# A two-block transformer kernel: the attention layers' stages put in another order

## The chip, the core and the metric

The kernel runs on one core of a Trainium2 chip. The time is the device time of the whole program in microseconds (us). The core has a matrix engine, TensorE (PE in the profile, its weight loads PEld), VectorE (DVE), ScalarE (ACT), GpSimd (POOL) and SyncE (SP), which here only issues DMAs. Each engine takes its own instructions strictly in the order in which they were written, and they meet through semaphores. TensorE writes to eight PSUM banks of 128 x 512 f32.

## What is computed

A sequence of 256 tokens of width 1024 goes through two layers of a first block (`_layer`, twice) and through a second block (retention, a SwiGLU, a short convolution, eight experts). Everything is f32. The change is inside `_layer`, ahead of its feed-forward part:

```python
xn = _rms(x, norm_mix_g)
z = xn @ w_in                       # 1024 x 7756 weights
(m_qk, m_v, m_o, m_if, s_q, s_ckv, i_q, i_k, i_w, d_q, d_k, d_v, g_pre) = _split_cols(z)
# branch a: mLSTM. Causal convolution and silu on m_qk, chunked decays from m_if,
y_a = sigmoid(m_o) * _rms(_mlstm(mq, mk, m_v, m_if + gate_b))
# branch b: sparse attention. 64 keys a query, chosen by an index score
kv = _rms(s_ckv) @ w_kv_up
y_b = _dsa(rope(_rms(s_q)), rope(_rms(kv_k)), kv_v, rope(i_q), rope(i_k), i_w)
# branch c: difference of two softmaxes
y_c = _rms(_diff_attn(rope(_rms(d_q)), rope(_rms(d_k)), d_v, lam)) * (1 - lam_init)
gates = sigmoid(g_pre + b_gate)     # three of 1024 columns
merged = sum(gates[i] * (y[i] @ w_branch[i]) for i in range(3))
x = x + merged @ w_out
```

## The kernel before

The program is one function, `build`, with a block of instructions for each engine. The order of each engine is written out by hand; nothing plans it. Tokens are tiled in two (`tt`) of 128. Weights come through a ring of six units of 1 MB that SP loads in the order of use and that waits for the unit six earlier to be read (`stream`, `unit_read`). `chunk` (L564) is the usual projection: two units, for each `tt` one bank and eight matmuls, then ScalarE copies the bank to `z` (`z_evac`). A gate chunk has one more matmul for its bias.

Banks go round: `fill(ALL)` takes the next of the eight and first waits until whoever was handed that bank eight fills ago has emptied it. `hand(ins, bank, who)` gives a filled bank to ScalarE or VectorE, which take theirs in that order. `point(name)` marks how many banks had been handed over, and others wait until all up to there are emptied. `transposes` (L448) turns four 128 x 128 tiles into one bank.

TensorE's order in a layer (`layer`, L706) before: `norm_transposes`; the eight columns of `m_if` from a small resident weight `w_if` (two groups of eight matmuls, 4 rows out); `m_qk` feature-major (two chunks); eight `z_chunks` (v, o, and six of 438 columns from s_q to d_v); two gate chunks; transposes of the normed `s_ckv`; the kv up-projection; two gate chunks; all of the mLSTM (`mlstm`, L852, ending with transposes of its output); transposes of the heads of s_q, k, d_q, d_k, i_q and i_k; the index scores; six banks of sparse scores; one gate chunk; transposes of the probabilities and products with the values; transposes of y_b; six banks of the differential scores; the last gate chunk; the differential weights' transposes and products; transposes of y_c; the three branch projections (L835 on); `w_out`; the feed-forward part.

VectorE's (`layer`, L1733): `mlstm_rows` and `convolve`; then, once ScalarE has emptied all z chunks (`point("z")`), the squares of s_q, d_q, d_k and s_ckv, one root for all, `rope` of s_q; `ckvT`; `rope` of d_q, d_k, i_q, i_k and of the keys; `mlstm`, which ends with `out_norm` and the product with the sigmoid; `top_keys` (L1686 on: sums the index scores, then eight rounds of MAX8 and MATCH_REPLACE8 for each `tt`); `scores` (mask, maximum, for each of six banks); the output of the sparse branch; `scores` again, the difference of the two softmaxes, `out_norm`; the merging of the branches. ScalarE evacuates banks, and takes the exponentials (`exps`), roots and, in one go at the end, the sigmoid of all 3072 gate columns. On ScalarE a change between functions such as Exp, Ln, Sqrt, Silu and Sigmoid shows as an ACT_TABLE_LOAD.

Of the kernel before, what the change touches and what calls it, by code (L numbers as in the profile page):

```python
# [10 lines left out]
ALU = mybir.AluOpType  # L11
ACT = mybir.ActivationFunctionType
AX = mybir.AxisListType

P = 128
# [30 lines left out]
PARAMS = 24  # L46
# [59 lines left out]
def build(nc, a, out):  # L106

    ctx = ExitStack()
    with ctx:
# [11 lines left out]
        w_if = sb("w_if", [P, DEPTH, KT, 8])  # L121
# [16 lines left out]
        rowf = ybuf[0:M_HEADS, 4 * SEQ:12 * SEQ].rearrange("p (r t) -> p r t", t=SEQ)  # L138
# [132 lines left out]
        sig_act = signal("sigmoids")  # L271
# [35 lines left out]
        gates_after = dict(z=2, kv=2, mlstm=0, dsa=1, diff=1)  # L307
# [22 lines left out]
        z_chunks = [(C_V, 512), (C_O, 512)] + [(C_SQ + 438 * i, 438) for i in range(6)]  # L330
        g_chunks = [(C_G + 512 * i, 512) for i in range(6)]
# [10 lines left out]
        def _(eng):  # L342
# [363 lines left out]
            def layer(li):  # L706
# [12 lines left out]
                for _, n in z_chunks:  # L719
                    chunk(n, "act")  # L720
                point("z")
                g_left = [list(range(6))]

                def gates(m):

                    for c in range(m):
                        i = g_left[0].pop(0)
                        pe_bias = li * 6 + i
                        chunk(512, "act", bias=pe_bias)

                gates(gates_after["z"])
# [15 lines left out]
                gates(gates_after["kv"])  # L747
                mlstm()
                gates(gates_after["mlstm"])

                eng.wait_ge(rope_dve.sem, pe.next(rope_dve))
                for col in (C_SQ, None, C_DQ, C_DK):
                    for half in range(2):
                        def src(i):
                            c = (2 * half + i // 2) * P
                            return kv[:, i % 2, c:c + P] if col is None else zc(i % 2, col + c, P)
                        transposes(src, 4, "act")
                transposes(lambda i: zc(i % 2, C_IQ + (i // 2) * P, P), 4, "act")
                transposes(lambda i: tmp[:, 3, i * P:(i + 1) * P], 2, "act")
                point("heads")  # L760
                eng.wait_ge(act_freed.sem, pe.point("heads", act_freed))

# [9 lines left out]
                for which in (0, 2):  # L772


                    for j in range(6):
# [7 lines left out]
                    if which == 0:  # L783
                        gates(gates_after["dsa"])

                        def turn_probs(j):
                            eng.wait_ge(prob_act.sem, 12 * li + j + 1)
                            transposes(lambda i: pbuf[:, j, i * P:(i + 1) * P], 4, "act")
                            point("pT")


                        turn_probs(0)
                        for j in range(6):
                            tt, _, hs = score_bank(j)
                            if j < 5:
                                turn_probs(j + 1)
                            if j in (0, 2):
                                bo = fill(ALL)
                            eng.wait_ge(act_freed.sem, pe.point("pT", act_freed))
                            for i, h in enumerate(hs):  # L800
                                for s in range(tt + 1):
                                    c = (i * (tt + 1) + s) * P
# [1401 lines left out]
```

## Time and profile before

| | |
|---|---|
| median of three runs | 2911.97 us (2903.65 to 2913.78) |
| the profiled execution | 2908.88 us |
| its span, first to last instruction | 2907.1 us |
| mean granted TensorE clock | 0.962 |
| PE busy | 2704.9 us (93%) |
| DVE, ACT, POOL busy | 1802.8, 1177.7, 231.9 us |
| DMA | 610 MB, 210 GB/s on average |
| first layer, from the first projection to the merged branches | 34 to 411 us |
| the same of the second layer | 655 to 1035 us |

The span is cut into stretches by time from its start. "Busy" of an engine is the time in which it had an instruction; the granted clock (PEclk) is the share of TensorE's full clock that it was given, 1.00 for 2.4 GHz and 0.50 for 1.2 GHz.

### The profile page before, as it was taken

What the parts mean: (1) busy time and instruction counts of PE and PEld (TensorE: products, weight loads), DVE (VectorE), ACT (ScalarE), POOL (GpSimd) and SP (SyncE); (2) the same over time, 40 slices, a digit from 0 to 9 for tenths busy, and PEclk for the clock granted to TensorE, in tenths of its full rate; (3) what the DMA queues carried; (4) which work ended last, traced back from release to release, by engine and by line L of the source; (5) the groups of instructions that cost most, each with busy time, mean ns of one, the idle gap of its engine ahead of it and who ended that gap; (6) DMA issues with size and microseconds to landing.
All of it is one profiled execution on the core that took longest, in us unless ns stands there. A gap on an engine that the chain in (4) does not pass through costs nothing.

```text
span 2907.1 us, 29086 instructions
## 1 busy us (share of the span) xinstructions
PE 2704.9 (93%) x11636; PEld 2037.4 (70%) x11636; DVE 1802.8 (62%) x1938; ACT 1177.7 (41%) x1325; POOL 231.9 (8%) x112
## 2 busy tenths in 40 slices
PE   5997898989997889989989989799999999999997
PEld 4445546876445448888768879687878778787876
DVE  2045525442065345555555447699999989999997
ACT  1112311011113310034620014577777777777775
POOL 0000003320000013300024320000000000000000
PEclk9998899999997899999999999899999999999999
DMA  5441135532430145545445535498989989898985
GB/s 161 139 158 58 58 116 174 201 132 101 164 130 30 58 161 186 201 140 177 157 148 207 193 120 186 146 381 311 381 318 361 338 323 372 313 382 315 376 328 195
DMA packets 276201, 610.10 MB, mean 210 GB/s; under 512 B 12670, under 2 KB 50228, under 8 KB 275904
## 3 DMA queue, kind: packets, MB, share of 16 engines
q1 hardware_dynamic: 276032, 607.64, 59.0%
q8 instruction: 131, 2.15, 0.3%
q14 instruction: 38, 0.31, 0.0%
HBM read 606.56 MB, written 1.05 MB: 209 GB/s over the span
## 4 chain that ended last, share of the span: by engine, by line
PE 83%; DVE 12%; ACT 3%; issue 1%; SPq 0%; DMA 0%; DVEq 0%; ACTq 0%
PE bank L418 81%; DVE split L1455 5%; PE bank L448 2%; PE bank L637 1%; DVE parts L1501 1%; ACT xs L1077 1%; DVE x_resid L1483 1%; DVE work L1712 0%; ACT split L1077 0%; DVE parts L1441 0%; DVE top L1711 0%; DVE tmp L1491 0%; ACT parts L1077 0%; SPq L2044 0%; ACT L1077 0%
## 5 line engine op out<-in xcount | busy, mean ns | idle before, releaser
L418 PE MATMUL bank<-split,parts 128*128 128x512 f32 (+1 forms) x6720 | 1539.7, 389 | 29.3 <-DVE parts L1441 13.1
L418 PEld LDWEIGHTS bank<-split,parts 128*128 128x128 f32 x6720 | 1247.7, 189 | 291.5 <-issue 19.8
L1455 DVE TENSOR_TENSOR split<-ring,split 128x2048 fp32r<-128x2048 f32 x444 | 1024.5, 2353 | 95.2 <-POOL split L2025 67.7
L1077 ACT ACTIVATE split<-ring 128x2048 fp32r<-128x2048 f32 x336 | 641.8, 1918 | 194.9 <-PE bank L418 194.9
L418 PE MATMUL bank<-ring,xnT 128*128 128x512 f32 (+1 forms) x1024 | 428.9, 578 | 1.8 <-ACT xnT L1077 1.8
L418 PEld LDWEIGHTS bank<-ring,xnT 128*128 128x128 f32 x1024 | 194.3, 192 | 234.2 <-issue 231.9
L2025 POOL TENSOR_SCALAR split<-ring 128x2048 fp32r<-128x2048 f32 x108 | 231.7, 2148 | 1477.6 <-DVE x_resid L1483 1114.3
L1077 ACT ACTIVATE parts<-bank 128x512 fp32r<-128x512 f32 x150 | 79.7, 583 | 390.5 <-PE bank L637 390.5
L1501 DVE TENSOR_TENSOR parts<-bank,parts 128x512 fp32r<-128x512 f32 x150 | 95.4, 678 | 144.3 <-ACT parts L1077 144.3
L1077 ACT ACTIVATE tmp<-bank 128x512 f32<-128x512 f32 x158 | 87.6, 586 | 203.6 <-PE bank L418 203.6
L1491 DVE TENSOR_TENSOR tmp<-bank,tmp 128x512 f32<-128x512 f32 x150 | 97.8, 679 | 115.7 <-PE bank L418 114.8
L1469 DVE TENSOR_TENSOR halves<-ring,halves 128x1024 fp32r<-128x1024 f32 x96 | 116.4, 1224 | 79.3 <-ACT halves L1077 78.8
L1077 ACT ACTIVATE halves<-ring 128x1024 fp32r<-128x1024 f32 x96 | 101.3, 1060 | 144.0 <-PE bank L418 144.0
L1077 ACT ACTIVATE z<-bank 128x512 f32<-128x512 f32 (+1 forms) x52 | 29.0, 566 | 223.6 <-PE bank L418 223.6
L418 PE MATMUL bank<-xparts,halves 128*128 128x256 f32 x960 | 116.8, 285 | 0.3 <-DVE xparts L1441 0.3
L418 PEld LDWEIGHTS bank<-xparts,halves 128*128 128x128 f32 x960 | 116.4, 193 | 0.9 <-issue 0.9
L1555 DVE TENSOR_TENSOR tmp<-z 128x512 f32<-128x512 f32 (+1 forms) x16 | 10.0, 626 | 156.2 <-ACT z L1077 155.8
L1483 DVE TENSOR_TENSOR x_resid<-bank,x_resid 128x512 f32<-128x512 f32 x60 | 41.3, 692 | 91.1 <-PE bank L418 91.1
L418 PE MATMUL bank<-ring,ybuf 128*128 128x512 f32 x192 | 88.4, 624 | 1.6 <-ACT ybuf L1077 1.6
L418 PE MATMUL bank<-halves,xparts 128*128 128x512 f32 x384 | 88.6, 391 | 0.0
L448 PE MATMUL bank<-const,xs 128*128 128x128 f32 x176 | 34.7, 378 | 55.1 <-ACT xs L1077 52.1
L418 PEld LDWEIGHTS bank<-halves,xparts 128*128 128x128 f32 x384 | 71.8, 188 | 15.1 <-issue 0.5
(233 smaller groups left out, 1619.9 us busy)
## 6 DMA issues: line engine op xcount, KB each, us to landing
ring<-in_moe_w_gate SPq DMA_DIRECT2D x112, 1024.0 KB, 7.9
ring<-in_moe_w_up SPq DMA_DIRECT2D x112, 1024.0 KB, 7.5
ring<-in_moe_w_down SPq DMA_DIRECT2D x112, 1024.0 KB, 7.5
ring<-in_w_gate_up SPq DMA_DIRECT2D x44, 1024.0 KB, 5.2
ring<-in_w_in SPq DMA_DIRECT2D x40, 1024.0 KB, 6.3
ring<-in_ret_w_in SPq DMA_DIRECT2D x24, 1024.0 KB, 5.1
ring<-in_w_down SPq DMA_DIRECT2D x22, 1024.0 KB, 5.0
ring<-in_w_in SPq DMA_DIRECT2D x24, 876.0 KB, 5.8
```

Source lines behind the costliest of these rows:

```text
L418: return nc.tensor.matmul(o, l, r, start=first, stop=final, **kw)
L448: ins = nc.tensor.transpose(bank[b][:, i * P:i * P + rows], src_of(i), ident[0:rows, 0:rows])
L637: return [nc.tensor.transpose(bank[b[tt]][:, f * P:(f + 1) * P], hb[:, tt, f * P:(f + 1) * P], ident) for f in range(n // P)]
L1077: return nc.scalar.activation(out, in_, func, **kw)
L1455: V.tensor_tensor(split[:, m % SPLITS, 1, :], ring[:, n % RING, :], split[:, m % SPLITS, 0, :].bitcast(F32), ALU.subtract).then_inc(low_ma ...
L1469: V.tensor_tensor(low, half_of(n, j, by_column), high.bitcast(F32), ALU.subtract).then_inc(half_low.sem, half_low.tick())
L1483: ins = V.tensor_tensor(o, b[:, :], o, ALU.add)
L1491: ins = V.tensor_tensor(hb[:, tt, 0:n], b[:, 0:n], sg[:, tt, 0:n], ALU.mult)
L1501: V.tensor_tensor(parts[:, 1, f, c], b[:, 0:n].rearrange("p (f t) -> p f t", t=P), parts[:, 0, f, c].bitcast(F32), ALU.subtract).then_inc( ...
L1555: then(V.tensor_tensor(sq, src, src, ALU.mult))
L2025: nc.gpsimd.tensor_scalar(split[:, m % SPLITS, 0, :], ring[:, n % RING, :], 1.0, 0.0, ALU.mult, ALU.add).then_inc(high_made.sem, high_made ...
```

## The change

Nothing is computed otherwise; the stages stand in another order on each engine, and some are cut finer.

The small weight `w_if` and its two loads go. The columns from `m_if` to `d_v` are now six chunks of 440 (436 the last), so that `m_if` comes out token-major with s_q, and four small matmuls against the identity turn it. The new order of TensorE in a layer is: m_qk; the chunk with s_ckv; the index chunk; transposes of normed s_ckv; the chunk with m_if and s_q; kv up-projection; `m_if` turned; index heads turned; v; index scores; o; sparse heads turned; chunk dq; sparse scores; chunks dk and dv; gates 1; probabilities and values of the sparse branch; the mLSTM's exponents and weights; y_b turned; differential heads turned; branch 1; the mLSTM's values; gates 0; y_a turned; differential scores; gates 2; differential products; branch 0; y_c turned; branch 2. VectorE norms and turns heads as each chunk comes, sums the index scores and chooses keys before it scans the mLSTM's rows, and merges a branch as it comes (`merge`). ScalarE takes the sigmoids straight from the banks (`z_evac` with a function). SP loads the weights in the new order.

```diff
-        w_if = sb("w_if", [P, DEPTH, KT, 8])
-        z_chunks = [(C_V, 512), (C_O, 512)] + [(C_SQ + 438 * i, 438) for i in range(6)]
-        g_chunks = [(C_G + 512 * i, 512) for i in range(6)]
+        z_v, z_o = (C_V, 512), (C_O, 512)
+        z_if_sq, z_ckv, z_index, z_dq, z_dk, z_dv = [(C_IF + 440 * i, min(440, C_G - C_IF - 440 * i)) for i in range(6)]
...
@@ tensor, layer @@
-                b = fill(ALL)
-                for g in range(2):
-                    for k in range(KT):
-                        ins = mm(bank[b][0:4, g * SEQ:(g + 1) * SEQ], w_if[:, li, k, 4 * g:4 * g + 4], xnT[:, k, :],
-                                 k == 0, k == KT - 1)
-                hand(ins, b, "dve")
...
+                columns(z_ckv, "ckv")
+                columns(z_index, "index")
                 eng.wait_ge(kvn_dve.sem, pe.next(kvn_dve))
                 transposes(lambda i: yb[:, i % 2, (i // 2) * P:(i // 2 + 1) * P], 4, "dve")
                 point("ckvT")
+                columns(z_if_sq, "sq")
...
+                eng.wait_ge(act_freed.sem, pe.point("sq", act_freed))
+                b = fill(ALL)
+                for g in range(2):
+                    for tt in range(TT):
+                        c = g * SEQ + tt * P
+                        ins = mm(bank[b][0:4, c:c + P], zc(tt, C_IF + 4 * g, 4), ident, True, True)
+                hand(ins, b, "dve")
...
+                columns(z_v, "v")
+                eng.wait_ge(act_freed.sem, pe.point("index heads", act_freed))
                 for tt in range(TT):
                     for odd in range(2):
                         b = fill(ALL)
...
+                columns(z_o, "o")
+                turn_heads(lambda tt, c: zc(tt, C_SQ + c, P), lambda tt, c: kv[:, tt, c:c + P])
+                columns(z_dq, "dq")
+                head_scores(0)
+                columns(z_dk, "dk")
+                columns(z_dv, "dv")
+                gates(1)
...
+                mlstm_weights()
+                eng.wait_ge(dve_freed.sem, pe.point("dsa", dve_freed))
+                turn_branch()
+                turn_heads(lambda tt, c: zc(tt, C_DQ + c, P), lambda tt, c: zc(tt, C_DK + c, P))
+                branch(1)
+                mlstm_values()
+                gates(0)
+                eng.wait_ge(yb_dve.sem, pe.next(yb_dve))
+                turn_branch()
+                head_scores(2)
+                gates(2)
+                eng.wait_ge(act_freed.sem, pe.point("dv", act_freed))
...
+                branch(0)
+                eng.wait_ge(yb_dve.sem, pe.next(yb_dve))
+                turn_branch()
+                branch(2)
@@ scalar, layer @@
+                z_evac(*z_ckv)
+                for f in range(KT):
+                    eng.wait_ge(conv_dve.sem, act.next(conv_dve))
+                    A(mqkT[:, f, :], mqkT[:, f, :], ACT.Silu).then_inc(silu_act.sem, silu_act.tick())
+                head_roots(24, 25)
+                z_evac(*z_index)
+                z_evac(*z_if_sq)
+                head_roots(0, 8)
...
+                z_evac(*z_o, ACT.Sigmoid)
+                turned_heads(0)
+                z_evac(*z_dq)
                 exps()
-                gates(gates_after["dsa"])
+                z_evac(*z_dk)
+                z_evac(*z_dv)
+                head_roots(8, 24)
+                gates(1)
...
-                for tt in range(TT):
-                    A(zc(tt, C_G, 3 * D), zc(tt, C_G, 3 * D), ACT.Sigmoid).then_inc(sig_act.sem, sig_act.tick())
@@ vector, layer @@
-                eng.wait_ge(act_freed.sem, dve.point("z", act_freed))
+                eng.wait_ge(act_freed.sem, dve.point("ckv", act_freed))
+                z_sums(((3, (C_CKV, 1, 256)),))
...
+                eng.wait_ge(act_freed.sem, dve.point("sq", act_freed))
+                z_sums(((0, (C_SQ, 8, HD)),))
+                mean_squares(z_heads(1, 0, 8), z_heads(0, 0, 8), HD)
+                z_inverse(0, 8)
+                rope_from_z(C_SQ, 0)
+                mlstm_rows(li)
                 eng.wait_ge(act_freed.sem, dve.point("kv", act_freed))
...
-                mlstm()
                 top_keys()
                 scores(lambda tt: msel[:, 0:P] if tt == 0 else msel[:, P:384])
+                mlstm_scans()
+                eng.wait_ge(act_freed.sem, dve.point("dq", act_freed))
+                z_sums(((1, (C_DQ, 8, HD)),))
+                eng.wait_ge(act_freed.sem, dve.point("dk", act_freed))
+                z_sums(((2, (C_DK, 8, HD)),))
...
+                mlstm_weights()
+                merge(1, True)
+                mlstm_values()
                 scores(lambda tt: const[:, K_DIAG:K_DIAG + P] if tt == 0 else causal2)
...
+                merge(0, False)
+                ins = merge(2, False)
@@ sync @@
-            for li in range(DEPTH):
-                load(w_if[:, li, :, :], a["w_in"][li, :, C_IF:C_IF + 8].rearrange("(k p) c -> p k c", p=P))
             load(w_rt[:, :, :], a["moe_router_2"].rearrange("(k p) c -> p k c", p=P))
...
+                for col, width in (z_ckv, z_index, z_if_sq):
                     columns(w_in, col, width)
-                gate_columns(gates_after["z"])
                 rows_of(a["dsa_w_kv_up"][li], 1)
+                for col, width in (z_v, z_o, z_dq, z_dk, z_dv):
+                    columns(w_in, col, width)
+                gates(1)
+                branch(1)
+                gates(0)
+                gates(2)
+                branch(0)
+                branch(2)
                 rows_of(a["w_out"][li], 4)
```

## Rows read from the trace of the kernel before

**Rows 1.** The page, part 1: busy time, share and instructions of each engine.
```profile
PE 2704.9 (93%) x11636; PEld 2037.4 (70%) x11636; DVE 1802.8 (62%) x1938; ACT 1177.7 (41%) x1325; POOL 231.9 (8%) x112
```

**Rows 2.** Waits of TensorE, 34 to 1036 us, both layers: total, times, longest.
```profile
PE bank L448 <- DVE yb L1684: 18.9, 2, 9.5
PE bank L418 <- DVE tmp L1699: 13.3, 2, 6.6
...
PE bank L448 <- DVE yb L1651: 11.4, 2, 5.7
PE bank L418 <- ACT pT L1077: 10.7, 8, 3.2
...
PE bank L418 <- ACT ikT L1077: 2.2, 2, 1.1
PE bank L418 <- DVE ckvT L1763: 2.1, 2, 1.0
...
PE bank L448 <- DVE yb L1789: 1.6, 2, 0.8
```

**Rows 3.** Windows: stretch, length, busy (instructions) of engines, PEclk, DMA share, GB/s.
```profile
240.00:244.50 4.50, 4.50 (x25) 3.36 (x23) 1.28 (x3) 2.61 (x4) 0.00 (x0) 1.00 0.65 208
244.50:259.20 14.70, 14.70 (x53) 12.34 (x52) 5.93 (x19) 2.85 (x4) 0.00 (x0) 0.54 0.19 79
268.70:272.00 3.30, 3.30 (x16) 3.30 (x17) 0.00 (x0) 2.13 (x5) 0.00 (x0) 0.52 0.00 0
272.00:281.30 9.30, 8.18 (x80) 7.52 (x78) 3.59 (x13) 5.73 (x11) 0.00 (x0) 1.00 0.01 2
288.00:296.00 8.00, 8.00 (x10) 3.03 (x11) 7.41 (x23) 0.00 (x0) 0.00 (x0) 0.51 0.00 0
312.20:333.00 20.80, 20.02 (x102) 19.50 (x103) 4.38 (x8) 5.55 (x17) 0.00 (x0) 0.52 0.14 56
350.00:357.00 7.00, 4.86 (x37) 3.95 (x35) 0.69 (x1) 3.50 (x5) 0.00 (x0) 1.00 0.82 298
362.70:369.00 6.30, 5.52 (x13) 3.06 (x14) 0.00 (x0) 4.99 (x4) 0.00 (x0) 0.50 0.01 4
...
936.70:957.30 20.60, 19.75 (x101) 19.26 (x103) 4.17 (x7) 5.39 (x16) 0.00 (x0) 0.52 0.14 56
```

**Rows 4.** Timeline of TensorE, first layer: start, length, instructions.
```profile
34.02 7.07 PE L418 MATMUL bank<-xnT,w_if 128*4 128x256 f32 x32 [1.06 <-DVE xnT L1420]
...
68.75 98.27 PE L418 MATMUL bank<-ring,xnT 128*128 128x512 f32 x256
166.94 1.12 PE L418 MATMUL bank<-bgate,const 12*128 12x512 f32 x2
...
272.90 2.35 PE L448 MATMUL bank<-const,z 128*128 128x128 f32 x20
...
365.41 44.16 PE L418 MATMUL bank<-ring,ybuf 128*128 128x512 f32 x96 [0.78 <-ACT ybuf L1077]
```

**Rows 5.** Timeline of ScalarE, first layer: one load of a function table.
```profile
83.29 1.28 ACT L1077 ACT_TABLE_LOAD   x1
```

**Rows 6.** Timeline of VectorE, first layer: row sums, norm and rope of keys, key selection.
```profile
41.44 0.46 DVE L1610 TENSOR_SCALAR ybuf<-bank,gateb 4x256 f32<-4x256 f32 x1
...
221.05 0.69 DVE L1555 TENSOR_TENSOR tmp<-xs 128x512 f32<-128x512 f32 x1
...
231.36 0.69 DVE L1576 TENSOR_TENSOR xs<-tmp 128x512 f32<-128x512 f32 x1
...
277.33 0.35 DVE L1699 TENSOR_SCALAR idx<-bank,iw 128x128 f32<-128x128 f32 x1 [8.70 <-PE bank L418]
...
287.35 0.48 DVE L1699 TENSOR_SCALAR tmp<-bank,iw 128x256 f32<-128x256 f32 x1
```

**Rows 7.** Timeline of SP at the start: issues of the last parameters.
```profile
9.89 2.31 SPq L2044 DMA_DIRECT2D w_if<-in_w_in x2
12.23 6.09 SPq L2044 DMA_DIRECT2D w_rt<-in_moe_router x1
```

**Rows 8.** Chain of waits at the start, and DMA packets from 18 to 20.3 us.
```profile
12.23 8.00 DMA w_rt<-in_moe_router
...
DMA packets 2669, 0.16 MB, mean 70 GB/s; under 512 B 2631, under 2 KB 2631, under 8 KB 2669
```

More of the change, by code:

```diff
@@ L45 @@
 HALVES = 4
-PARAMS = 24
+PARAMS = 22
 GROUPS = D_FF // HALF
@@ L718, in layer, with columns, gates @@
                     point("qk")
[L719 to L731, printed above, removed]
+                def columns(z_chunk, name=None):
+                    chunk(z_chunk[1], "act")
+                    if name:
+                        point(name)
+                def gates(branch):
+                    for i in range(2):
+                        chunk(512, "act", bias=6 * li + 2 * branch + i)
+                    point("gates")
+                columns(z_ckv, "ckv")
+                columns(z_index, "index")
                 eng.wait_ge(kvn_dve.sem, pe.next(kvn_dve))
@@ L771, in layer, with turn_heads, head_scores @@
                         hand(ins, b, "dve")
-                for which in (0, 2):
+                def turn_heads(q_of, k_of):
+                    eng.wait_ge(rope_dve.sem, pe.next(rope_dve, 2))
+                    for of in (q_of, k_of):
+                        for half in range(2):
+                            transposes(lambda i: of(i % 2, (2 * half + i // 2) * P), 4, "act")
+                    point("heads")
+                def head_scores(which):
+                    eng.wait_ge(act_freed.sem, pe.point("heads", act_freed))
                     for j in range(6):
@@ L828, in layer, with branch @@
                                    "act")
[L829 to L833 removed]
+                    point("branch")
+                def branch(br):
+                    eng.wait_ge(act_freed.sem, pe.point("branch", act_freed))
                     views = [take((2, 1024)), take((2, 1024))]
@@ L884, in mlstm @@
                     hand(ins, b, "dve")
-                eng.wait_ge(yb_dve.sem, pe.next(yb_dve))
-                for half in range(2):
-                    transposes(lambda i: yb[:, i % 2, (2 * half + i // 2) * P:(2 * half + i // 2 + 1) * P], 4, "act")
             for li in range(DEPTH):
@@ L1256, in layer, with gates, head_roots @@
-                copy(iqT[:, :, :].rearrange("p f t -> p (f t)"))
-                copy(ikT[:, :], SEQ)
+                        b = take()
+                        A(zc(tt, col, n), b[:, 0:n], func).then_inc(act_freed.sem, act_freed.tick())
+                def gates(branch):
+                    for i in range(2):
+                        z_evac(C_G + (2 * branch + i) * HALF, HALF, ACT.Sigmoid)
+                def head_roots(lo, hi):
+                    o, i = (hsum[:, r, kA:kB].rearrange("p (t c) -> p t c", t=TT)[:, :, lo:hi] for r in (2, 1))
+                    roots(o, i)
@@ L1259, in exps, with turned_heads @@
+                def turned_heads(first):
+                    for w in (first, first + 1):
+                        for half in range(2):
+                            copy(hT4[:, w, 2 * half:2 * half + 2, :].rearrange("p f t -> p (f t)"))
                 def exps():
@@ new lines, in z_sums, with z_inverse, rope_from_z @@
+                def z_sums(cols):
+                    for tt in range(TT):
+                        o = kA + 25 * tt
+                        for i, (col, nh, w) in cols:
+                            heads_sum(heads(zc(tt, col, nh * w), nh), nh, w, hsum[:, 0, o + 8 * i:o + 8 * i + nh])
+                def z_inverse(lo, hi):
+                    eng.wait_ge(root.sem, dve.next(root))
+                    then(V.reciprocal(z_heads(3, lo, hi), z_heads(2, lo, hi)))
+                def rope_from_z(col, i):
+                    for tt in range(TT):
+                        c = kA + 25 * tt + 8 * i
+                        rope(zc(tt, col, 512), 8, tt, hsum[:, 3, c:c + 8], qk_gain[:, (0, 2, 3)[i], li, :],
+                             done=rope_dve if tt else None)
```

292 lines of the change are left out of this document (121 added, 171 removed).

## The prediction

> **What bounds the kernel now.** I read the page first: TensorE is busy 93% of the span and no other engine is above 62% [rows 1], so a change that leaves the arithmetic alone can only win where TensorE waits, where its clock is low, or where its work goes. The page's slices put nearly all of the low ones in the two attention stretches, 34 to 411 and 655 to 1035 us. There I read, in this order, the list of TensorE's waits, which names each and its releaser; the windows, for the granted clock; and the timelines of TensorE, VectorE and SP, to lay out the new order by the durations of the old. The rest of the program isn't touched, and I carry it over unchanged.
>
> The reader should see two losses of about the same size. The first is waiting. Per layer TensorE waits 9.5 us for the mLSTM's output norm, 6.6 us for a bank that VectorE still holds while it sums the index scores (L1699), 5.7 us for the norm of the differential output, 3.2 us for the first probabilities, and 1.1, 1.0 and 0.8 us for smaller things [rows 2]. The second is the clock. It is at 1.2 GHz (0.50 to 0.54) in five stretches of the first layer [rows 3], and the second layer has their twins, one of which stands there, at 0.52 in 936.7 to 957.3 us.
>
> **Part 1: the waits.** The sum over both layers of those that the new order covers is 18.9 + 13.3 + 11.4 + 2.2 + 2.1 + 1.6 = 49.5 us, and of the 10.7 us on `pT` the two first ones, 6.4 us, so 55.9 us or **28.0 a layer** [rows 2]. What covers each in the new order:
> - mLSTM output norm (9.5): `mlstm_values` is followed by gates 0, two chunks. A chunk of 512 costs 98.27 us / 3652 columns x 512 = 13.8 us (eight z chunks are 2 x 512 + 6 x 438 columns), and with two biases of 1.1 us a gate chunk is 16 us, so the pair covers with 32 us a VectorE chain that is under 12.
> - differential output norm (5.7): branch 0 stands there, a third of 44.16 us [rows 4], under 14 at full clock.
> - first probabilities (3.2): three stages stand between scores and probabilities (dk, dv, gates 1), some 56 us.
> - `ckvT`, `ikT`, y_b (2.9 together): a projection or the mLSTM's weights follow each.
> - the differential weights: they were hidden behind one gate chunk but for the `pT` copies; now two chunks stand there.
>
> The three later `pT` waits (0.7 each), the wait of 0.8 us for the last branch's transposes and that of 1.5 us for the merge stay.
>
> **Part 2: the bank.** The 6.6 us come from the ring of eight banks. The index scores' four banks are VectorE's, and the third is free only once it reaches L1699 of the second token tile, 287.35 + 0.48 - 277.33 = 10.5 us after it begins [rows 6]. In the new order the fill that meets this bank is the first of chunk dq. From the end of the s_q chunk TensorE needs until then: kv up-projection 7.1, m_if turned 0.9, index heads 0.7, v 13.8, index scores 1.4, o 13.8, sixteen transposes 1.9 (2.35 us for 20 [rows 4]), in all 39.6 us. VectorE needs from the same moment: evacuation 0.6, norm and rope of s_q 11.0 (the same work as 221.05 to 232.05 on the keys), three operations on four rows, 1.4, norm and rope of the keys 11.0, about 2 for three table loads that ScalarE has ahead of that root (1.28 each [rows 5], part of it under the sums), and the 10.5 [rows 6]: 36.5 us. So there are 3 us to spare, and I count no wait. It is the tightest place of the new order; each microsecond that VectorE is later than that would be one of TensorE, twice. The other chains have more: the heads of the sparse branch are ready 11 us early, the differential ones 30.
>
> **Part 3: the clock.** TensorE time lost to 1.2 GHz a layer is busy time x (1 - clock): 14.70 x 0.46 + 3.30 x 0.48 + 8.00 x 0.49 + 20.02 x 0.48 + 5.52 x 0.50 = **24.6 us** [rows 3]. Three of these stretches follow a wait that goes: those at 288 and 362.7 follow waits of 6.6 and 5.7 us and hold dense work, and 312.2 begins behind the 3.2. But the first, 244.5 to 259.2, follows none: TensorE was busy for all of 240 to 244.5, with the mLSTM's four-row matmuls, and the clock fell. So not everything comes back. In the new order the sparse probabilities and values, the mLSTM's weights, and 24 transposes follow one another: at full clock 7.3 (half of the 12.9 us of their stage inside 312.2 to 333, and one set of transposes), 9.5 (four heads of 2.3 us and the rows' transpose), 0.9 and 1.9 us. Counting from the row, the mLSTM's weights hold the full clock for about 4.5 us; the other 5 cost double, the transposes after it 1.6 more (as in 268.7 to 272), and some of branch 1 perhaps runs low, up to half of 4 us: **8 us a layer come back as a new loss**. Bounds: none, if the clock holds, and 16, if it falls already under the probabilities (3.3 + 9.5 + 3). I take 8 because that is what the only row with such matmuls behind a dense stage shows; behind the new small stages elsewhere (index scores, heads, differential products) I take none, since like ones ran at 1.00 in 272 to 281.3 and 350 to 357.
>
> The Trainium skill, "TensorE: Matmul & The Clock Gate", section "HAM oscillation — how this bites in real kernels", names gaps in which the array is idle as what gates the clock. By that the new stretch, which has no gap, would keep 2.4 GHz, and the loss of 8 would be none; the row at 240 to 244.5, busy throughout and followed by 0.54, speaks against it [rows 3].
>
> **Part 4: work removed.** The 32 instructions on `w_if` take 7.07 us [rows 4], in the second layer too, apart from the clock there, which the next stage would take over. In their place come eight instructions of a transpose's size, 0.9 us (bounds 0.5 to 1.6: 2.35 us for 20, and double), and eight more columns, 0.2 us. **6.0 us a layer.**
>
> **Part 5: ScalarE and DMA.** With sigmoids taken per stage, ScalarE changes its function table 15 times a layer where it did 10 times: 5 x 1.28 = 6.4 us more [rows 5]. I cost them at nothing: ScalarE is idle for most of a layer, and the two that lie on a chain (ahead of the keys' root) are in part 2. The Trainium skill, "ScalarE: Activation LUTs", section "Table sets: the hidden batching unit", asks for calls to be batched by set, which the change undoes; if each stood in TensorE's way it would cost 12.8 us in all, and the sum would be that much worse. The SP queue issues the same units in a new order, the ring stays six deep, and no wait of TensorE in rows 2 is for weights; nothing.
>
> **Part 6: the start.** Nothing starts until the last parameter has landed, at 20.2 us, 8.00 us after the issue of the router weights [rows 8]. The two `w_if` loads before them take 2.31 us of SP's queue [rows 7] and are, like the router's, made of 32-byte pieces, 1024 each. The router's issue moves up by 2.3 us; 2048 pieces fewer at the rate of 18 to 20.3 us (2631 in 2.3) give 1.8 more: **4.1 us**. Bounds: 0, if other parameters decide, and 7.6, if the 8.00 us shrink by two thirds.
>
> **The sum.** 4.1 + 2 x (28.0 + 24.6 + 6.0 - 8) = 4.1 + 2 x 50.6 = 105.3 us. The profiled execution took 2908.88 us, 1.8 more than its span, and gives 2803.6. It lies 3.1 us below the median of the runs, 2911.97, by which the forecast is 2806.7: I say 2806.
>
> **Rivals.**
> - *The clock holds* (the page's rule): 2 x 8 us better, about 2790. For it: dense work now stands on both sides. Against it: the row at 240 to 244.5.
> - *The clock falls early*, under the sparse probabilities: 2 x 8 worse, about 2822. For it: in 312.2 to 333 the same stage, TensorE busy, stayed at 0.52 for its whole length. Against: it entered that stage behind a wait.
> - *The bank's wait only moves* to chunk dq, or the change doesn't cover what it says elsewhere: VectorE 6 us later than in part 2 costs 3 us a layer, and 10 later 7; 2812 to 2820.
> - *Slower than before*: the clock falls in the stretch of small matmuls and stays at 1.2 GHz through the dense stages behind it. From gates 1 to the merge there are 145 us of TensorE work at full clock in a layer; all of it low costs 145 and gives 2909 + 2 x (145 - 59) = 3081. It decides once some 117 us a layer run low that I count as full. Against it: dense chunks that began low were at full clock within 8 us each time [rows 3].
>
> **Chances.** Forecast (8 or near) 0.52, clock holds 0.13, falls early 0.22, bank and other new waits 0.10, slower 0.01, nothing gained that can be measured (gains given back in ways I don't see) 0.02. The best combination is 7.6 + 2 x 58.6 = 125 us, 2787; falling early with the start at 0 and 3 us of bank gives 2 x (58.6 - 19) = 79, 2833. With a little for the durations read from one execution: 2784 to 2838. A measurement of this kernel can tell about 0.5%, some 15 us, from no change, so faster 0.97, same 0.02, slower 0.01.
>
> **What would show it.** TensorE's waits on L1684, L1651 and L1699 are gone and its idle time in a layer is under 6 us; the span from first projection to merged branches is about 327 us (377 less 50) in each layer. The granted clock is 1.00 up to the end of gates 1, then falls a few microseconds into the mLSTM's weights and is back within branch 1. No `w_if`, and the first transposes begin near 25 us. A wait on a bank ahead of chunk dq, a stall inside the mLSTM's weights, or a low clock in a dense chunk would make me wrong.

## The result, and the profile after

The changed kernel takes **2803.77 us**, median of four runs (2802.98 to 2807.95), against 2910.43 for the kernel before on the same chip: a ratio of 0.9639, 95% interval 0.9619 to 0.9660. The profiled execution took 2802.98 us, with a span of 2801.2 and a mean granted clock of 0.979. The forecast was 2806, the range 2784 to 2838.

The page after, part 1, columns as in [rows 1]:

```profile
PE 2653.2 (95%) x11588; PEld 2003.4 (72%) x11588; DVE 1803.6 (64%) x1944; ACT 1175.2 (42%) x1329; POOL 231.9 (8%) x112
```

TensorE has 48 instructions fewer and is busy for 51.7 us less, by work removed and by the clock; the other engines are where they were. TensorE's waits after, from 25 to 1000 us, both layers (total, times, longest); they answer [rows 2]:

```profile
PE bank L446 <- ACT xs L1092: 28.3, 4, 8.3
...
PE bank L416 <- ACT pT L1092: 5.0, 8, 0.7
PE bank L416 <- ACT xnT L1092: 3.8, 4, 1.0
PE bank L446 <- DVE xs L1842: 3.0, 2, 1.5
PE bank L416 <- ACT ybuf L1092: 1.8, 2, 0.9
```

The 18.9, the 13.3 and the 11.4 us of the kernel before have no line any more. The 28.3 and the 3.8 belong to the norms ahead of the projections and of the feed-forward part, outside the stretch that the change reorders. Inside a layer there remain 2.5 us on `pT`, 1.5 for the merge and 0.9 for the last branch, 4.9 in all.

Timeline of TensorE after, where each layer begins and where its branches are merged (start, length, instructions, and in brackets the wait before them):

```profile
34.62 27.86 PE L416 MATMUL bank<-xnT,ring 128*128 128x256 f32 x128 [1.02 <-ACT xnT L1092]
...
359.93 1.97 PE L446 MATMUL bank<-const,xs 128*128 128x128 f32 x16 [1.51 <-DVE xs L1842]
...
605.41 30.24 PE L416 MATMUL bank<-xnT,ring 128*128 128x256 f32 x128 [1.02 <-ACT xnT L1092]
...
933.09 1.97 PE L446 MATMUL bank<-const,xs 128*128 128x128 f32 x16 [1.51 <-DVE xs L1842]
```

The first layer's stretch is 359.93 - 34.62 = 325.3 us (before 377.1), the second's 327.7 (before 379.4): 51.7 us saved in each. That is 103.5 of the 105.9 us between the two spans. The second layer has a slow first projection in this execution, 30.24 us for 27.86; without it 54.1 us would be saved there. The start is 0.6 us later, the first feed-forward part 0.3 longer, and the untouched rest after the second layer takes 1868.1 us instead of 1871.4. Those 3.3 us aren't the change's: that rest took from 1867.9 to 1871.6 us in the executions below.

Windows of the first layer after, columns as in [rows 3]:

```profile
217.70:220.50 2.80, 2.80 (x16) 2.34 (x16) 1.32 (x3) 0.89 (x3) 0.00 (x0) 1.00 0.00 1
220.50:222.30 1.80, 1.80 (x9) 1.39 (x8) 0.56 (x1) 0.09 (x1) 0.00 (x0) 0.67 0.00 0
222.30:232.50 10.20, 10.20 (x29) 8.01 (x29) 2.79 (x5) 1.57 (x3) 0.00 (x0) 0.50 0.00 0
232.50:234.30 1.80, 1.80 (x11) 1.80 (x10) 0.56 (x1) 0.64 (x2) 0.00 (x0) 0.50 0.00 0
234.30:236.30 2.00, 2.00 (x18) 2.00 (x17) 0.00 (x0) 1.80 (x6) 0.00 (x0) 0.89 0.03 8
236.30:250.00 13.70, 13.70 (x35) 6.05 (x34) 2.08 (x3) 2.20 (x3) 0.00 (x0) 1.00 0.00 0
```

This is the one stretch of the layer behind its first projection that still runs at 1.2 GHz. TensorE is busy in all of it. It holds the four-row matmuls of the mLSTM's exponents, in 217.7 to 232.5, and the transposes behind them.

### The profile page after: what moved, and what is told of

Its sections match the earlier page's. It is cut to its first block, busy times and chain, and to the rows that moved or that the text cites. A ratio compares the mean times of both kernels' runs of the same rounds, so it can differ in the third digit from the quotient of the medians.

```text
span 2801.2 us, 29018 instructions
## 1 busy us (share of the span) xinstructions
PE 2653.2 (95%) x11588; PEld 2003.4 (72%) x11588; DVE 1803.6 (64%) x1944; ACT 1175.2 (42%) x1329; POOL 231.9 (8%) x112
## 4 chain that ended last, share of the span: by engine, by line
PE 86%; DVE 10%; ACT 3%; issue 1%; DMA 0%; SPq 0%; DVEq 0%; ACTq 0%
PE bank L416 84%; DVE split L1468 6%; PE bank L446 1%; DVE parts L1514 1%; PE bank L635 1%; ACT xs L1092 1%; DVE x_resid L1496 1%; ACT split L1092 0%; DVE parts L1454 0%; DVE tmp L1504 0%; DMA w_rt<-in_moe_router 0%; ACT parts L1092 0%; SPq L2086 0%; ACT L1092 0%; DVE xs L1438 0%
## 5 line engine op out<-in xcount | busy, mean ns | idle before, releaser
L416 PE MATMUL bank<-split,parts 128*128 128x512 f32 (+1 forms) x6720 | 1539.2, 389 | 29.1 <-DVE parts L1454 12.8
L416 PE MATMUL bank<-ring,xnT 128*128 128x512 f32 (+2 forms) x1024 | 425.5, 572 | 1.8 <-ACT xnT L1092 1.8
L1092 ACT ACTIVATE z<-bank 128x512 f32<-128x512 f32 (+2 forms) x52 | 29.6, 569 | 268.5 <-PE bank L416 268.4
L446 PEld LDWEIGHTS bank<-const,xs 128*128 128x128 f32 x176 | 30.9, 200 | 60.6 <-ACT xs L1092 56.0
```

The source lines that it names most:

```text
L416: return nc.tensor.matmul(o, l, r, start=first, stop=final, **kw)
L446: ins = nc.tensor.transpose(bank[b][:, i * P:i * P + rows], src_of(i), ident[0:rows, 0:rows])
L1092: return nc.scalar.activation(out, in_, func, **kw)
```

## The experiments

Each kernel is the changed one with one edit, except where another is named. "Layer" is the stretch from the first projection to the merged branches.

### What lowers the clock in the mLSTM's weights

TensorE never waits in the stretch shown above, and yet the clock falls. My theory named the matmuls themselves: the exponents are built by matmuls that contract over four partitions, one for each head. The experiment gives them 128 partitions, of which 124 hold zeros, and leaves their number and their columns alone.

```diff
-                    sel = ident[0:4, h:h + 1]
+                    sel = ident[:, h:h + 1]
@@ twice a bank: @@
-                        mm(..., rowf[:, ROW_KEY, s * P:(s + 1) * P], sel.broadcast_to([4, n]), True, False)
+                        mm(..., rowp[:, ROW_KEY, s * P:(s + 1) * P], sel.broadcast_to([P, n]), True, False)
```

> The changed kernel, but the mLSTM's 32 exponent matmuls a layer contract over all 128 partitions instead of 4 (the selecting operand is a column of the 128-row identity, so the other rows are multiplied by zero and the result is the same). Number, columns and order of the instructions stay. Theory 'few rows': the clock falls in the mLSTM's weights because most of its TensorE time is on four-row matmuls, which leave the array nearly idle. Then the clock stays at 1.00 from the sparse probabilities to branch 1, the stretch from the first probabilities' transposes to branch 1 shrinks from 27.0 to 20.4 us, and the time falls by 2 x 6.6 = 13 us, to about 2791. Rival 'small instructions': it falls because the instructions are short and weight loads lie between them, whatever their rows. Then the stretch stays at 27 us and the time at 2804.

Measured: **2787.06 us** (2785.16 to 2788.70), ratio 0.9592 (0.9563 to 0.9622). Windows of this kernel over the same stage, and one bank's matmuls in TensorE's timeline:

```profile
217.70:220.50 2.80, 2.80 (x18) 2.54 (x18) 1.32 (x3) 0.80 (x3) 0.00 (x0) 1.00 0.00 0
220.50:222.30 1.80, 1.80 (x13) 1.67 (x12) 1.12 (x2) 0.35 (x2) 0.00 (x0) 1.00 0.00 0
222.30:229.00 6.70, 6.70 (x50) 6.17 (x49) 2.79 (x5) 3.81 (x10) 0.00 (x0) 1.00 0.01 2
```

```profile
217.94 0.70 PE L417 MATMUL bank<-const,ybuf 128*128 128x256 f32 x2
218.48 0.59 PE L417 MATMUL bank<-ybuf,const 128*128 128x256 f32 x2
...
225.91 1.04 PE L447 MATMUL bank<-const,yb 128*128 128x128 f32 x8
226.78 1.91 PE L447 MATMUL bank<-const,z 128*128 128x128 f32 x16
228.53 2.74 PE L417 MATMUL bank<-ring,ybuf 128*128 128x512 f32 x6
```

Two matmuls of 256 columns last the same with 128 rows as with four (0.70 and 0.59 us, against 0.68 and 0.59 in the changed kernel's rows below), and the clock stays at 2.4 GHz. From the probabilities' transposes at 209.21 to branch 1 at 228.53 are 19.3 us instead of 27.0 (209.22 to 236.26): 7.7 us in each layer, 15.4 of the 16.7 between the medians. So the four-row form is what brought the clock down here, with TensorE never idle. The stretch was expected to shrink to 20.4 us only. The rest isn't the clock: one head of the mLSTM takes 2.33 us with four rows while the clock is still full (217.89 to 220.22 in the changed kernel) and 1.97 with 128 (220.01 to 221.98). Timeline of the changed kernel:

```profile
217.89 0.68 PE L416 MATMUL bank<-const,ybuf 4*128 4x256 f32 x2
218.41 0.59 PE L416 MATMUL bank<-ybuf,const 4*128 4x256 f32 x2
...
220.22 0.70 PE L416 MATMUL bank<-const,ybuf 4*128 4x256 f32 x2
```

Not tried is whether other row counts between 4 and 128 hold the clock, or whether it is the change between four-row and 128-row matmuls that lowers it.

The same edit in the kernel before asks whether the whole new loss was already there.

```diff
@@ kernel before, two lines like the ones above @@
-                    sel = ident[0:4, h:h + 1]
+                    sel = ident[:, h:h + 1]
```

> The kernel before the change with the exponents' contraction over 128 rows, nothing else. By the theory 'few rows' the clock stays at 1.00 through the mLSTM's weights there too: of the loss in 244.5 to 259.2 (6.8 us a layer) nearly all goes, 2 x 6 to 7 = 12 to 14 us, so about 2895, and the five waits and the low clocks behind them stay. Rival: the clock fell there for the idle time of TensorE's neighbours or by chance of place; then 2907.

Measured: 2888.14 us (2881.68 to 2900.52), ratio 0.9943 (0.9915 to 0.9971), which is 8 to 25 us less. Timeline and waits (34 to 1000 us) of this kernel:

```profile
240.76 0.70 PE L419 MATMUL bank<-const,ybuf 128*128 128x256 f32 x2
...
248.73 2.85 PE L419 MATMUL bank<-v_ext,pbuf 128*128 128x129 f32 x24
262.38 1.97 PE L449 MATMUL bank<-const,yb 128*128 128x128 f32 x8 [10.80 <-DVE yb L1686]
```

```profile
PE bank L449 <- DVE yb L1686: 21.6, 2, 10.8
```

The mLSTM's matmuls end at 251.6 us instead of 259.2. The wait for its output norm behind them grows from 9.5 to 10.8 us, and the clock still falls in that wait. The first layer gains 6.3 us. The second gains 13.1. The sparse stage ran at 0.52 in both layers of the kernel before [rows 3]. Here it has 0.52 again in the first layer (305.9 to 326.7 us), but in the second the clock came back inside it, at about 931 us. Why it did so only there I did not settle. The eleven executions of the kernel before on this chip lie at 2894 to 2898 us or at 2908 to 2912, the six of this kernel between 2882 and 2900, so such a step can be chance of the execution. The estimate of 12 to 14 us holds for twice the first layer's 6.3; what lies above it isn't shown to be the edit's.

### What the covers are worth

The mLSTM's output norm is hidden behind gates 0. The experiment puts gates 0 ahead of the mLSTM's values again, on TensorE and in ScalarE's order.

```diff
-                mlstm_values()
                 gates(0)
+                mlstm_values()
```

> The changed kernel with one cover taken away: gates 0 stand before the mLSTM's values instead of behind them, so nothing lies between the values and the transposes of their normed output. By the prediction (part 1 and 3) the wait of the kernel before comes back, 9.5 us a layer, and behind it the clock is low again for the transposes and scores that follow and some of gates 2 (kernel before: 1.6 us in the transposes behind this wait, up to 4 in dense work): 11 to 14 us a layer, 22 to 28 in all, 2826 to 2832. Rival: the VectorE chain was partly hidden in other ways, or gates 2 take up the delay elsewhere, since VectorE and ScalarE are then less pressed later; then under 10 us in all come back.

Measured: **2833.25 us** (2828.12 to 2834.74), ratio 0.9748 (0.9715 to 0.9782), 29.5 us more than the changed kernel. Timeline and windows:

```profile
298.12 1.97 PE L446 MATMUL bank<-const,yb 128*128 128x128 f32 x8 [10.09 <-DVE yb L1697]
300.02 5.11 PE L416 MATMUL bank<-qkbuf 64*128 64x128 f32 x32
```

```profile
298.00:302.00 4.00, 3.88 (x20) 0.50 0.01 4
302.00:305.00 3.00, 3.00 (x23) 0.74 0.00 0
305.00:312.00 7.00, 7.00 (x17) 1.00 0.00 0
```

(Here the windows show TensorE alone: length, busy, clock, DMA share, GB/s.) The wait is back at 10.1 us, and behind it come 0.9 us in the transposes (1.97 instead of 1.04) and 1.7 in the scores (5.11 instead of 3.44) for the low clock. In the second layer the scores take 6.32 us. From branch 1 to gates 2, the part that the edit touches, are 66.1 and 67.3 us instead of 53.2, so the cover of a 10.1 us wait is worth 12.9 and 14.1 us (expected: 11 to 14).

The whole layers are 16.1 and 11.7 us longer. The difference lies in places that the edit doesn't touch. The first layer has 1.6 in a slower first projection (29.47 us instead of 27.86) and 1.7 because the clock fell sooner in the mLSTM's weights. The second has a first projection of 27.86 us where the changed kernel's execution had 30.24.

### How tight the bank is ahead of chunk dq

VectorE must read the third bank of index scores before TensorE may fill it with chunk dq. Timeline of VectorE and of TensorE in the changed kernel:

```profile
132.77 0.48 DVE L1712 TENSOR_SCALAR tmp<-bank,iw 128x256 f32<-128x256 f32 x1
```

```profile
136.99 1.04 PE L446 MATMUL bank<-const,xs 128*128 128x128 f32 x8
137.86 11.98 PE L416 MATMUL bank<-ring,xnT 128*128 128x440 f32 x32
```

The bank was read at 133.25 and chunk dq began at 137.86, without a wait: 4.6 us to spare. The two experiments make VectorE late ahead of `top_keys` with additions of 0.7 us whose result is not used: five, or eleven.

```diff
+                for _ in range(5):        # 11 in the other
+                    then(V.tensor_tensor(tmp[:, 0, :], tmp[:, 1, :], tmp[:, 1, :], ALU.add))
                 top_keys()
```

> The changed kernel with five VectorE additions on 128 x 512 (0.72 us each, 3.6 us) put ahead of the key selection in each layer. In the changed kernel the third index-score bank is emptied at 133.2 us and chunk dq needs it at 137.9 us, so 4.6 us are to spare (3 by the prediction). If that bank is the next limit, 3.6 us cost nothing: no wait of TensorE on the line of the index sums, the layer as long as without. Rival: other consumers of VectorE's later work are tighter, and 1 us or more of it shows in the layer's length.

> As before, with eleven additions, 7.9 us a layer. By the bank: 7.9 - 4.6 = 3.3 us of waiting at chunk dq in each layer, named after the index sums' line, and no other new wait; the layer 3.3 us longer. Rival: the bank isn't the limit, and no wait stands there, or the full 7.9 come through.

Measured, one execution each: 2802.91 us with five, no new wait; 2815.13 with eleven. Waits (25 to 1000 us), timeline and TensorE's windows with eleven:

```profile
PE bank L416 <- DVE tmp L1712: 6.7, 2, 3.4
```

```profile
143.31 13.74 PE L416 MATMUL bank<-ring,xnT 128*128 128x440 f32 x32 [3.35 <-DVE tmp L1712]
```

```profile
143.00:147.00 4.00, 3.69 (x6) 0.64 0.42 155
147.00:151.00 4.00, 4.00 (x12) 0.93 0.00 0
```

Eleven additions are some 8.0 us (0.69 and a short gap each), less the 4.6 to spare 3.4: the wait is 3.35. It doesn't come alone. The chunk of 11.98 us takes 13.74 behind it, since the clock fell in the wait. From the transposes ahead of the chunk to the scores behind it are 18.1 us instead of 12.8, in both layers, so that 3.35 us of waiting cost 5.3, where 3.3 were expected. Twice that is 10.6 of the 12.2 us. Most of the rest is in parts that the edit doesn't touch: the first projections (29.58 us instead of 27.86 in the first layer, 27.86 instead of 30.24 in the second), and in the second layer 1.6 us because the clock fell already in the first head of the mLSTM's weights.

### What the start waits for

The first matmul after starts at 21.02 us, where the kernel before has 20.27. Chain of waits of the changed kernel at the start (start, length, what), and the issues in SP's timeline:

```profile
9.92 11.06 DMA w_rt<-in_moe_router
```

```profile
9.92 0.40 SPq L2086 DMA_DIRECT2D w_rt<-in_moe_router  x1
10.36 10.40 SPq L2112 DMA_DIRECT2D ring<-in_w_in  x4
```

The router's weights are issued at 9.92 instead of 12.23 us [rows 8], and take 11.06 us to land instead of 8.00. Four kernels ask why. One puts the two loads of `w_if` back, without using them:

```diff
+            for li in range(DEPTH):
+                load(w_if[:, li, :, :], a["w_in"][li, :, C_IF:C_IF + 8].rearrange("(k p) c -> p k c", p=P))
             load(w_rt[:, :, :], a["moe_router_2"].rearrange("(k p) c -> p k c", p=P))
```

> The changed kernel with the two loads of the small m_if weight put back (they are not used). By the prediction's part 6 the removal of their 2048 pieces was worth 4.1 us: then the start would be at 25 us. By what the two traces show it was worth nothing, as the start is set by pieces that share the engines with the first weight units: then it is at 20 to 22 us.

Measured, one execution: 2803.00 us, first matmul at 20.70. Taking the two loads out gained nothing. That is a net result: with them back, the ring's first weights are issued at 18.89 us instead of 10.36, so what the small pieces cost can't be told here from what weights close behind cost. The next takes the router's load out of the parameters and issues it in the second block, where its weights are used; the third issues it ahead of all other parameters.

```diff
@@ router late @@
-            load(w_rt[:, :, :], a["moe_router_2"].rearrange("(k p) c -> p k c", p=P))
@@ later on SP, with a semaphore of its own @@
+            eng.dma_start(w_rt[:, :, :], a["moe_router_2"].rearrange("(k p) c -> p k c", p=P)).then_inc(routed.sem, routed.tick(16))
@@ router first @@
+            load(w_rt[:, :, :], a["moe_router_2"].rearrange("(k p) c -> p k c", p=P))
             for name, r0, nr, t in (("norm_mix_g", G_MIX, 16, 0), ...
```

> The changed kernel, but the router's weights, not needed before the experts, are no longer among the parameters on which the start waits; they are loaded after the two layers' weights. The changed kernel started its first transposes at 21.0 us, not 4 us before the 20.3 of the kernel before as forecast. Theory 'queued behind': the router's 1024 small pieces were issued 2.3 us earlier, at 9.9 us, but the first six weight units of 1 MB follow at once and share the DMA engines, so that they land late. Then without it the start waits for the last of the large parameters only, and TensorE begins at 14 to 16 us: 5 to 7 us less, 2797 to 2799. Rival 'something else lands last near 20 us' (the small broadcast gains or the gate biases): the first transposes stay at 20 to 21 us and the time at 2804.

> The changed kernel with the load of the router's weights as the first of all instead of the last parameter. 'Queued behind': the small pieces pass through empty DMA engines, and the first transposes begin at 14 to 17 us, near those of the kernel that loads them late. 'Small pieces cost their own time wherever they stand': they delay all that follows, and the start is at 20 to 21 us as now.

Measured: router late 2802.79 us (2798.83 to 2803.07), ratio 0.9642 (0.9612 to 0.9673), not to be told from the change; first matmul at 19.42. Router first, one execution: 2801.22 us, first matmul at 18.87. Neither start is where either theory put it (14 to 17 or 20 to 21 us): moving the router's load gains 1.6 and 2.2 us. In both another load has taken the router's place as the last; the chains of waits:

```profile
9.54 9.83 DMA bgate<-in_b_gate
```

```profile
10.16 8.66 DMA bgate<-in_b_gate
```

These are biases of 24 KB; in the fourth kernel, below, the same load takes 5.02 us. So something else makes them late. The candidates that I tried are the five loads that spread one row of gains or of the lambda vectors over 128 partitions. The fourth kernel has the router late and reads those five from rows of `x` instead, a row of its own for each partition. It leaves out the gains and lambdas, and only its start is read.

```diff
-                load(qk_gain[:, i, :, :], a[name].partition_broadcast(P))
-            load(lamv[:, :, :, :], a["diff_lambda"].partition_broadcast(P))
+                load(qk_gain[:, i, :, :], a["x"][0, 0:P, i * 128:(i + 1) * 128].rearrange("p (l d) -> p l d", l=DEPTH))
+            load(lamv[:, :, :, :], a["x"][0, P:2 * P, 0:512].rearrange("p (l a d) -> p l a d", l=DEPTH, a=4))
```

> The kernel that loads the router late, and besides takes the four head gains and the lambda vectors, of the same size, from rows of x instead of broadcasting one row over 128 partitions. It computes with wrong gains, so only its start is read. In the runs so far the last parameter, the gate biases, lands at 19 us though it is issued at 9.5, and between 12 and 16 us the DMA engines are busy while they move only some 50 GB/s in some 500 packets. Theory 'broadcasts': these packets all read the same addresses and are slow each; without them the biases land at 13 to 15 us and the first transposes begin then, 4 to 6 us earlier than in the router-late kernel (19.4). Rival 'shared engines': the bandwidth is lost to the weight units issued behind; then the start stays at 18 to 20 us.

Measured, one execution: 2796.73 us, and its last parameter:

```profile
9.61 5.02 DMA bgate<-in_b_gate
```

First matmul at 14.68 us, 4.7 earlier than with the router late alone. DMA packets from 12 to 20 us, first with the router late, then with the five loads changed too:

```profile
DMA packets 914, 1.13 MB, mean 141 GB/s; under 512 B 92, under 2 KB 453, under 8 KB 914
```

```profile
DMA packets 1862, 2.96 MB, mean 370 GB/s; under 512 B 129, under 2 KB 518, under 8 KB 1862
```

These are totals of all loads under way, the ring's weights among them. In the same 8 us 2.96 MB move instead of 1.13, with the engines busy in both (DMA share 1.04 and 0.96). The five loads have the same bytes and the same piece sizes in both kernels; what differs is that each partition's piece has its own address in HBM. So the spreading loads make late what stands behind them, by 4.7 us here. How they do it isn't shown. With the router first the DMA engines were busy for only 0.60 of these 8 us, and for 0.22 of 14 to 16 us, and the biases still landed at 18.8.

The Trainium skill, "DMA: Bandwidth & Descriptors", section "Why small descriptors are slow (HBM only)", puts the loss on a fixed cost for each small piece. That cost is the same in both kernels here, so it doesn't explain these 4.7 us, and 2048 pieces of 32 bytes fewer gained nothing on balance.

### All together

The last kernel has the 128-row exponents, the router late, the gains and lambdas loaded as one row and spread by a matmul against ones, and in the differential products the transposes one step ahead of the products, to take away the three `pT` waits of 0.7 us.

```diff
+            for r in (3, 2):
+                b = fill(ALL)
+                hand(mm(bank[b][:, :], ones[0:1, :], pbuf[0:1, r, :], True, True), b, "dve")
...
+                turn_diff(0)
+                for j, (tt, jj) in enumerate(((0, 0), (1, 0), (1, 1))):
+                    if j < 2:
+                        turn_diff(j + 1)
...
-                load(qk_gain[:, i, :, :], a[name].partition_broadcast(P))
+                load(pbuf[0:1, 2, i * P:(i + 1) * P], a[name].rearrange("(o l) d -> o (l d)", o=1))
```

> The changed kernel with four things: the 128-row exponents; the router loaded late; the head gains and lambda vectors loaded as one row each and spread over the partitions by a matmul with a row of ones, so that no broadcasting load is left; and the differential branch's transposes issued one set ahead of the products. From the runs: 2787.1 (128 rows), less 3.5 to 5.5 for the start (first transposes at 14.7 us instead of 21.0 in the run without broadcasts, less 1 to 2 for the two matmuls and copies ahead of the first norm), less 2 x 1.5 for two of the three pT waits: 2779. Rival: the gains don't add, since the time saved at the start only lets TensorE wait for its first weight units; then 2784.

Measured: **2778.10 us** (2777.26 to 2780.10, five runs), ratio 0.9558 (0.9531 to 0.9584). Timeline of TensorE: the start, the differential products, the end of the first layer.

```profile
13.82 0.47 PE L701 MATMUL bank<-const,pbuf 126*128 126x126 f32 x1 [13.82 <-DMA bgate<-in_b_gate]
...
29.61 30.14 PE L418 MATMUL bank<-xnT,ring 128*128 128x256 f32 x128 [1.01 <-ACT xnT L1104]
...
312.80 1.13 PE L418 MATMUL bank<-z,pT 128*128 128x128 f32 x8 [0.39 <-ACT pT L1104]
313.77 0.60 PE L448 MATMUL bank<-const,pbuf 128*128 128x128 f32 x4
314.20 2.01 PE L418 MATMUL bank<-z,pT 128*128 128x128 f32 x16
...
347.25 1.96 PE L448 MATMUL bank<-const,xs 128*128 128x128 f32 x16 [1.51 <-DVE xs L1859]
```

The first matmul comes 7.2 us earlier than in the changed kernel and the first projection 5.0, since the spreading by matmul and its copies take some of it back. The layer is 317.6 us, as with the 128-row exponents alone, but its first projection took 30.1 us where there it took 27.9; without that the transposes one step ahead are worth 2.2 us a layer (1.5 expected). The gains add up, as expected: the sum was 2779, the rival 2784. This kernel is faster than both kernels of the case, by 26 us than the change, 0.9%.

## Why the prediction was right, point by point

**The waits (part 1): right.** All that I held for covered is gone, and none came back elsewhere but 0.39 us ahead of the first sparse product, which I had not counted. 4.9 us of idle time are left in a layer (forecast: under 6). Undoing one cover brings its wait back at full size, so this wait was covered and not just moved; the other covers were not undone one by one.

**The bank (part 2): right, with the margin too small.** 4.6 us to spare, not 3: VectorE ended about 1.6 us earlier than laid out, for the most part as the keys' root waited 0.8 us for ScalarE's function tables and not 2. The delays bear out both the margin and what lies behind it. My price for this rival was too low, though: 3.35 us of bank wait cost 5.3 a layer through the clock.

**The clock (part 3): mechanism right, size 8 for 6.6.** The losses behind the waits are all regained. The new loss is where I put it: the clock fell some 3 us into the mLSTM's weights, behind 220.5. The forecast of 4.5 was counted from the start of a window; the mLSTM's matmuls in the kernel before begin at 240.47, so its own row says 4.0. The clock was back in the last transposes ahead of branch 1 (0.89 in 234.3 to 236.3), which lost nothing and for which I had counted part of up to 2 us. At full clock the stretch of 27.0 us would be about 20.4, so 6.6 are lost. Two rivals are settled by the same rows. The clock did not fall under the probabilities (1.00 up to 220.5). Nor did it hold: the Trainium skill, "TensorE: Matmul & The Clock Gate", section "HAM oscillation — how this bites in real kernels", names idle gaps only, and by that this stretch would have kept 2.4 GHz; the trace disagrees, with 0.50 for 12.0 us in which TensorE was busy throughout. With 128 rows in place of four the same stretch does hold the clock, at 2787 us, near the 2790 that I had worked out for a clock that holds.

**Work removed (part 4): right.** `w_if`'s 32 instructions are gone, and `m_if` turned took 0.97 us until the next instruction (forecast 0.9), in TensorE's timeline:

```profile
105.16 1.04 PE L416 MATMUL bank<-const,z 128*4 128x128 f32 x8
```

**ScalarE and DMA (part 5): right.** ScalarE loads 15 tables in the first layer's stretch where it loaded 10, and no wait of TensorE for ScalarE grew by one.

**The start (part 6): wrong, 4.1 us forecast, none measured.** The step that failed was to take the last load in the chain for the cause of its own lateness, and to price it by its pieces: "the router's issue moves up by 2.3 us; 2048 pieces fewer ... give 1.8 more". The runs showed in its place that the load which lands last is made late by others: with the router's out of the way the biases landed at 18.8 to 19.4 us, and at 14.6 once the spreading loads were changed too. The router's own, issued 2.3 us earlier, landed 0.75 us later; whether the first weights of the ring, now issued closer behind it, did that wasn't tried. The bound of 0 was the case that held.

**The sum.** Two layers gave 103.5 us for the 101.2 of the sum, mostly the 1.4 us less of new loss in each. In the second a slow first projection took 2.4 back, and the columns of `m_if` gave that much more than 7.07 us (9.38 in the kernel before, at the low clock). The start gave -0.6 us for 4.1, the untouched rest 3.3 us for nothing. So 105.9 measured against 105.3 forecast is closer than the parts were: an error of 4.7 at the start was made good by 2.3 in the layers and 3.0 that no part of the change explains. The closeness is luck in that part.

**A slip in a rival.** "Slower than before" counts 145 us of TensorE work from gates 1 to the merge. The first layer after has 183.1 us there, 4.9 of them waiting and 6.6 clock, so about 171. All of it low would have given some 3130 us and not 3081. Nothing rests on it, as the dense stages kept the full clock.

## What to carry to other kernels

When stages are put in another order, count what each wait costs with the clock behind it: 3.35 us of waiting cost 5.3 here, and so a cover is worth more than the wait it hides, and a margin of a few microseconds on a shared bank is worth laying out engine by engine. Where the clock falls while TensorE is busy, look at the form of the matmuls; here zero rows up to 128 cost no time and gave 15.4 us back. The last item in a chain of waits tells who was late, not who made it late: move it, and see what takes its place.

## What the runs showed of the hardware that I had not expected

- The clock fell from 1.00 to 0.50 under uninterrupted work, in matmuls that contract over four partitions; with 128 partitions, pairs of 256 columns taking 0.59 us at full clock in both, it stayed at 1.00.
- While five loads that give 128 partitions the same row of HBM were under way, all DMA traffic from 12 to 20 us came to 141 GB/s; with loads of as many bytes from distinct rows it came to 370.
- The first projection of a layer, behind the wait for the norm, takes either 27.9 or 29.5 to 30.2 us, in one execution too (after, 27.86 us in the first layer and 30.24 in the second). In the long case its first microseconds run at half rate; the windows of TensorE in the second layer of the changed kernel say so:

```profile
605.00:609.00 4.00, 3.59 (x9) 0.50 0.00 0
609.00:614.00 5.00, 5.00 (x22) 0.88 0.02 3
```

In the first layer of the last kernel the same 4 us had half as many matmuls as usual (10 for 19) while the records gave 1.00, so there the recorded clock doesn't seem to follow what TensorE did. What decides between the two cases stays open.
